# Value products with the values as weights, in two column groups, and attention outputs kept transposed

## What is computed

```python
def sb_block(q, q_pos, k, v, k_pos):
    z = jnp.einsum('bqhd,bkhd->bhqk', q, k) * SB_HD ** -0.5
    mask = (k_pos[None, :] < q_pos[:, None])[None, None]
    log_beta = jax.nn.log_sigmoid(z)
    l = jnp.where(mask, jax.nn.log_sigmoid(-z), 0.0)
    c = lax.cumsum(l, axis=3, reverse=True) - l
    w = jnp.where(mask, jnp.exp(log_beta + c), 0.0)
    return jnp.einsum('bhqk,bkhd->bqhd', w, v)
...
    mix = jnp.concatenate([og, o_sb.reshape(B, T, SB_WIDTH)], axis=-1).astype(x.dtype)
    h = x + mix @ w_out
    u = rmsnorm(h, norm2_g).astype(x.dtype) @ w_up
    return h + jnp.square(jax.nn.relu(u)) @ w_down
```

## Time and profile before

| | |
|---|---|
| median of 3 runs | 3177.38 us (3176.07 to 3178.87) |
| the profiled execution | 3173.07 us, with a span of 3171.3 us |
| PE busy | 3076.5 us of the span |
| DVE, ACT, POOL busy | 1893.9, 1693.8, 1107.1 us |
| value products, line 1471 | 2256 records, from 859.8 to 2844.7 us |
| mean granted clock | 0.986 |

### The profile page before, as it was taken

One profiled execution on the slowest core, in us unless ns is written; L12 is line 12 of the kernel. 1 busy time (PEld: TensorE's weight loads), 2 busy tenths in 40 slices (PEclk: granted clock), 3 DMA queues, 4 the chain that ended last, 5 costly groups with the idle time before them and its releaser, 6 DMA issues. The chain is left out here.

```text
span 3171.3 us, 48786 instructions
## 1 busy us (share of the span) xinstructions
PE 3076.5 (97%) x18258; PEld 2640.2 (83%) x18258; DVE 1893.9 (60%) x3388; ACT 1693.8 (53%) x3148; POOL 1107.1 (35%) x642
## 2 busy tenths in 40 slices
PE   6999999999779999999999999999999999999999
PEld 5887788877679989888888988888898888889998
DVE  2565646546446666566665776777757667653333
ACT  3443434443357766555555666666556655543443
POOL 0331513215135663333333232222333333334665
PEclk9999999999779999999999999999999999999999
DMA  4654645544455554323333323222233333333443
GB/s 148 185 176 140 193 132 161 155 138 114 147 156 176 182 177 128 113 86 104 101 91 115 107 97 99 91 92 89 81 126 115 133 98 102 98 99 120 133 145 111
DMA packets 310747, 400.66 MB, mean 126 GB/s; under 512 B 70433, under 2 KB 225074, under 8 KB 309490
## 3 DMA queue, kind: packets, MB, share of 16 engines
q1 hardware_dynamic: 310514, 397.55, 40.1%
HBM read 339.95 MB, written 57.54 MB: 125 GB/s over the span
## 5 line engine op out<-in xcount | busy, mean ns | idle before, releaser
L1861 POOL TENSOR_TENSOR st_ul<-st_ur,st_uh 128x1024 fp32r<-128x1024 f32 x180 | 428.8, 2404 | 803.4 <-ACT st_uh L1669 803.4
L1868 POOL TENSOR_TENSOR st_dl<-st_dr,st_dh 128x1024 fp32r<-128x1024 f32 x180 | 430.9, 2415 | 610.4 <-ACT st_dh L1679 610.4
L1835 DVE TENSOR_TENSOR st_ya<-st_ya,st_dp 128x512 f32<-128x512 f32 x544 | 368.6, 681 | 97.2 <-PE st_dp L1589 96.0
L1636 ACT ACTIVATE st_a<-st_z 128x512 f32<-128x512 f32 (+3 forms) x336 | 177.2, 527 | 380.9 <-PE st_z L1448 252.7
L1761 DVE TENSOR_TENSOR_SCAN st_g<-st_z,st_g,st_a 128x511 f32<-128x511 f32 (+3 forms) x336 | 371.0, 1104 | 15.6 <-DVE st_g L1754 0.5
L1822 DVE TENSOR_TENSOR st_tl<-st_dp,st_th 128x512 fp32r<-128x512 f32 (+2 forms) x168 | 96.8, 576 | 437.6 <-ACT st_dp L1717 437.5
L1589 PE MATMUL st_dp<-st_dh,st_th 128*128 128x512 f32 x1020 | 336.9, 402 | 0.7 <-DVE st_ya L1835 0.6
L1589 PE MATMUL st_dp<-st_dh,st_tl 128*128 128x512 f32 x1020 | 336.9, 401 | 0.0
L1589 PE MATMUL st_dp<-st_dl,st_th 128*128 128x512 f32 x1020 | 334.5, 399 | 0.0
L1471 PEld LDWEIGHTS st_po<-st_v,st_wt 128*128 128x128 f32 x2256 | 303.3, 194 | 36.2 <-DMA st_v<-out_new_v 7.6
L495 PE MATMUL fr_pj<-fr_wl,fr_xh 128*128 128x512 f32 x816 | 330.3, 405 | 0.0
(11 more groups left out here) (165 smaller groups left out, 5738.6 us busy)
## 6 DMA issues: line engine op xcount, KB each, us to landing
st_ur<-in_w_up SPq DMA_DIRECT2D x75, 1024.0 KB, 5.3
st_dr<-in_w_down SPq DMA_DIRECT2D x75, 1024.0 KB, 4.9
fr_wr<-in_w_in SPq DMA_DIRECT2D x96, 512.0 KB, 4.0
st_ur<-in_w_out SPq DMA_DIRECT2D x10, 1024.0 KB, 5.0
st_dr<-in_w_out SPq DMA_DIRECT2D x10, 1024.0 KB, 5.0
fr_xb<-in_x SPq DMA_DIRECT2D x17, 512.0 KB, 4.5
st_ya<-in_x SPq DMA_DIRECT2D x17, 512.0 KB, 7.3
out_y<-st_ya SPq DMA_DIRECT2D x16, 512.0 KB, 3.9
```

Source lines behind the costliest of these rows:

```text
L1835: dve.tensor_tensor(part, part, dp[:, k % BANKS], ALU.add).then_inc(s_fd, 1)
L1861: pool.tensor_tensor(ul[:, c], ur[:, c], raw(uh[:, c]), ALU.subtract).then_inc(s_ul, 1)
L1868: pool.tensor_tensor(dl[:, k], dr[:, k], raw(dh[:, k]), ALU.subtract).then_inc(s_dl, 1)
```

## The change

`values` swaps the operands: `v` is stationary (128 keys x 64 columns) and `wt` moves (128 keys x 128 queries), so `po` now holds 64 columns x 128 queries, transposed. Key tile c writes partitions 0 to 63 when c is even and 64 to 127 when it is odd (the array's two column groups), and the two halves are added afterwards. A pair with a single key tile does it twice, once per half. ACT's `output` becomes `other_half`: for head h it copies the half that does not lie at the partitions of h's place (parity of h) into `mv`. A new `output` on DVE adds the half still in `po` to `mv` and writes it to `mT`, already transposed, at that place. `s_of`, for which PE's next pair waits, now comes from DVE. `mix_tile` transposes `mg` only; ACT and DVE read the second half of `xh` and `xl` from `mT`, and `out_tile` waits for that by `s_ml`. `MG` goes from 4 to 3 buffers.

```diff
@@ settings and plan
-MG = 4
+MG = 3
...
-                for a in range(2):
+                for a in range(1 if kind == "mix" else 2):
...
@@ tensor, values(u)
                 for c in range(un.n):
-                    mm = pe.matmul(po[:, tt % 2 * HD:(tt % 2 + 1) * HD], wt[:, u % 3, c * P:(c + 1) * P],
-                                   v[:, p, un.e * jobs[un.job].keys + un.lo + c],
-                                   start=(un.first and c == 0), stop=(un.last and c == un.n - 1))
+                    for half in range(2) if un.first and un.last and un.n == 1 else (c % 2,):
+                        mm = pe.matmul(po[64 * half:64 * half + 64, tt % 2], v[:, p, un.e * jobs[un.job].keys + un.lo + c],
+                                       wt[:, u % 3, c * P:(c + 1) * P], start=(tt, half) not in begun, stop=(un.last and c >= un.n - 2))
+                        begun.add((tt, half))
                 mm.then_inc(s_pv, 1)
...
@@ tensor, out_tile
                 if gg == 0:
-                    pe.wait_ge(s_fd, plan.full("mix", b, j, 1))
+                    pe.wait_ge(s_fd, plan.full("mix", b, j, 0))
+                    pe.wait_ge(s_ml, rows_before[b] + j + 1)
...
@@ scalar, part 2 of u(3)
-            def output(u):
+            def other_half(u):
                 un = units[u]
                 if un.last:
                     tt = tiles_done[u]
-                    b = jobs[un.job].block
+                    q = un.h % 2
                     act.wait_ge(s_pv, u + 1)
-                    if b and tt == outs_done(b - 1):
-                        act.wait_ge(s_full, plan.full("mix", b - 1, MTS[b - 1] - 1, 1))
-                    act.activation(ms[:, un.tile, un.h * HD:(un.h + 1) * HD], po[:, tt % 2 * HD:(tt % 2 + 1) * HD], ACT.Copy).then_inc(s_of, 1)
+                    if tt >= 2:
+                        act.wait_ge(s_of, tt - 1)
+                    act.activation(mv[64 * q:64 * q + 64, tt % 2], po[64 - 64 * q:128 - 64 * q, tt % 2], ACT.Copy).then_inc(s_oc, 1)
...
@@ scalar, high_halves (second half of a mix tile)
+                                yield plan.done("mix", b, j, 0) + 1
+                                act.wait_ge(s_of, outs_done(b))
+                                act.activation(xh[:, 4:8, j * P:(j + 1) * P], mT[:, :, j * P:(j + 1) * P], ACT.Copy).then_inc(s_hi, 1)
...
@@ vector
+            def output(u):
+                un = units[u]
+                if un.last:
+                    tt = tiles_done[u]
+                    b = jobs[un.job].block
+                    q = un.h % 2
+                    dve.wait_ge(s_oc, tt + 1)
+                    if b and tt == outs_done(b - 1):
+                        dve.wait_ge(s_ml, rows_before[b])
+                    ps = slice(64 * q, 64 * q + 64)
+                    dst = mT[ps, un.h // 2, un.tile * P:(un.tile + 1) * P]
+                    if un.first and un.n == 1:
+                        dve.tensor_copy(dst, po[ps, tt % 2]).then_inc(s_of, 1)
+                    else:
+                        dve.tensor_tensor(dst, po[ps, tt % 2], mv[ps, tt % 2], ALU.add).then_inc(s_of, 1)
...
             def part0(u):
+                if u(4) is not None:
+                    output(u(4))
                 if u(2) is not None:
                     transposed(u(2))
```

More of the change, by code:

```diff
@@ L1190, in __init__ @@
         first = [self.start[self.use["mix", b, 0, 0]] for b in range(MB)]
-        last = [self.end[self.use["mix", b, 1 if b else MTS[0] - 1, 1]] for b in range(MB)]
+        last = [self.end[self.use["mix", b, 1 if b else MTS[0] - 1, 0]] for b in range(MB)]
         self.region = [(-100e3, 0.0)] + [(last[b], first[b + 1]) for b in range(MB - 1)]
@@ L1256, in phase_stream @@
         wt = m.sb("wt", [P, 3, 512])
-        ms = m.sb("ms", [P, MT, 512])
+        mT = m.sb("mT", [P, 4, MT * P])
+        mv = m.sb("mv", [P, 2, P])
         mg = m.sb("mg", [P, MG, 512])
@@ L1273, in phase_stream @@
         tp = m.ps("tp", [P, 512])
-        po = m.ps("po", [P, 512])
+        po = m.ps("po", [P, 2, P])
         dp = m.ps("dp", [P, BANKS, 512])
@@ L1279, in phase_stream @@
         s_gb = m.sem("gb")
+        s_oc, s_ml = m.sem("oc"), m.sem("ml")
         s_kq, s_v = m.sems("kq", 2), m.sems("v", 2)
@@ L1459, in transposes @@
                 mm.then_inc(s_tr, 1)
+            begun = set()
             def values(u):
@@ L1481, in mix_tile @@
                 t = rows_before[b] + j
[L1482 to L1493, removed]
+                k = plan.use["mix", b, j, 0]
+                yield plan.start[k]
+                free(k)
+                pe.wait_ge(s_mg[t % MG], 16 * (t // MG + 1))
+                for c in range(4):
+                    mm = pe.transpose(dp[:, k % BANKS, c * P:(c + 1) * P], mg[:, t % MG, c * P:(c + 1) * P], idt[:])
+                mm.then_inc(s_full, 1)
             def out_tile(b, gg, j):
@@ L1684, in high_halves @@
                         for a2 in range(2):
+                            if kind == "mix" and a2:
+                                yield plan.done("mix", b, j, 0) + 1
+                                act.wait_ge(s_of, outs_done(b))
+                                act.activation(xh[:, 4:8, j * P:(j + 1) * P], mT[:, :, j * P:(j + 1) * P], ACT.Copy).then_inc(s_hi, 1)
+                                continue
                             k = plan.use[kind, b, j, a2]
@@ L1728, in part2 @@
                 if u(3) is not None:
-                    output(u(3))
+                    other_half(u(3))
                 if u(-1) is not None:
@@ L1780, in low_halves @@
                         for a2 in range(2):
+                            n += 1
+                            if kind == "mix" and a2:
+                                yield plan.done("mix", b, j, 0) + 1
+                                dve.wait_ge(s_hi, n)
+                                dve.tensor_tensor(xl[:, 4:8, j * P:(j + 1) * P], mT[:, :, j * P:(j + 1) * P],
+                                                  raw(xh[:, 4:8, j * P:(j + 1) * P]), ALU.subtract).then_inc(s_ml, 1)
+                                continue
                             k = plan.use[kind, b, j, a2]
-                            n += 1
                             yield plan.end[k]
```

## The result

| | before | with the change |
|---|---|---|
| median of 4 runs | 3177.2 us | 3224.6 us (3221.8 to 3234.9) |
| ratio | 1 | 1.0155, 95% interval 1.0132 to 1.0177 |
| span of the profiled execution | 3171.3 us | 3222.2 us |

What follows compares the result with a forecast made beforehand. PE, in flight 97% of the span, was taken to bound the kernel. The terms -8.5 - 7.5 + 32 + 10 + 2 = +28 us on 3173.1 gave 3201 us, and with 4.3 us for the median 3205 us, range 3185 to 3225.

Steps and rivals of the forecast that it cites:

- Value groups: Value products on PE, blocks 1 to 4: 0.78 us a unit for 4 or 3 key tiles, 0.56 for fewer; -8.5 us.
- the switch: On PE, each value group pays 0.34 us for going from the whole array to parts of it and back.
- rival 3: Value products on PE: no switch cost with all 128 rows in use; about -85 us in all, 3092 us; chance 0.10.
- Transposes: Mix stages on PE: 17 mix tiles lose four transposes each, 0.43 to 0.44 us a group; -7.5 us.
- The new wait: Pair starts in blocks 1 to 4: PE's values wait for DVE's late addition; +32 us, bounds nothing and 47.
- Rival 1: Pair starts: DVE is in time, so its additions make PE wait little; near -10 us, 3167 us; chance 0.17.
- Block 0: Block 0's attention at half clock: waits for DVE at seven of 16 pairs and dearer value units; +10 us, bounds 3 and 13.
- MG = 3: Mix stages: a block's fourth mix tile's load waits for the first one's transposes; +2 us, bounds 0 and 5.

Runs made afterwards that it cites:

- a_half: The changed kernel with every key tile on the first column half, ACT copying that half and DVE only moving it: 3330 us in a single run, ratio 1.0496.
- a_pair: a_best with the values of two units in one group, every second slot, on PE, ACT and DVE: 3127.8 us, ratio 0.9853 to the kernel before.
- a_load: The changed kernel with the mix load of a block's fourth tile sent to an idle third of hn and issued early: ratio 1.0081 to the kernel before.
- a_best: The changed kernel with both the load edit of a_load and the copy edit of a_copy: ratio 0.9981 to the kernel before, from 11 runs.
- b_mg3: The kernel before with only MG changed from 4 to 3 buffers: ratio 1.0052, +16.5 us in the medians.
- b_dve: The kernel before with the copy of po to ms moved from ACT, part 2, to DVE, part 0 of the next slot: ratio 1.0125, +36.6 us in the medians.
- a_copy: The changed kernel with po emptied by ACT alone in part 2, PE waiting for that, and DVE adding afterwards: ratio 1.0055 to the kernel before.

## Why the prediction was right in sign and short in size

- **Value groups: right.** 0.78 and 0.56 us a unit were forecast and measured, for every size of unit. That the columns work side by side was taken from the earlier trace rows; a_half shows it. That the switch is paid on 128 rows too, so that rival 3 falls, is in the two groups above, and a_pair, with half as many switches, gets back most of what they cost.
- **Transposes: right.** -7.5 was forecast for 17 tiles, 6.6 of it for the 15 in the mix stages of the table, and a_load's are 7.3 us shorter with a wait that accounts for 0.6.
- **The new wait: right.** "Of the 40 us I take 0.8, +32 us." Rival 1 falls: in blocks 1 to 4 PE stands 24.9 us for the addition and 4.6 us with no engine named. What it costs was measured three times: 36.6 us when it is put alone into the kernel before, 32 us back when it is taken out of the change, and again 0.0100, 32 us, with the load repaired (a_load to a_best). Of the 24.9 us at least 15.6 lie in block 3; the prediction had 24.9 of its 40 us there.
- **Block 0: oversized.** +10 was forecast, the stage became 3.1 us longer (44.7 to 47.8), the lower bound given. PE does wait 9.2 us for DVE there, seven times as forecast. But before it had waited 5.4 us for ACT, 5.1 of it at the place where it now waits 4.3 for DVE, and the wait for the load of `st_v` became 0.8 us shorter.
- **MG = 3: the step that failed.** "I take **+2 us**, bounds 0 and 5; in blocks 2 and 3 three down tiles lie between and cover it." It measured 21.6 us in the mix stages and 23 us in the ratios (a_load). The prediction reckoned landing from the moment the load may leave, and left out SP's queue: there the load stands behind a weight load that waits for POOL, and behind five loads of attention. So it left 8 us late in block 1, and 8 to 9 us late in blocks 2 and 3, where the three down tiles don't cover it; PE waited 9.9, 5.0 and 6.2 us.
- **The clock in blocks 1 to 4: left out.** The sum has no term for it. By stages it forecast +10 us for block 0, -5 for the mix stages and +23.5 for the attention stretches; the changed kernel's trace has +3.1, +14.3 and +34.0. So the attention stretches missed by 10 us of their own, though the prices of their groups and the wait came out as forecast. From 946 us on the granted clock in them is 0.50 for 26.0 us in five pieces, three behind the waits for `st_mg`, one in a wait for the addition and one behind a wait for `st_xl`; in the kernel before it is 1.00 there all the time. That is worth up to 13 us (an estimate: half of the 26.0). The misses of the three stages, +19, +10 and -7 us, are the profiled execution's, 51 us where 28 were forecast. The sign rests on the new wait, which was right; that the sum came nearer than its two short terms is luck, since block 0, too high by 7 us, took part of them back.
- **What stays open.** Attention stretches of a_best are 2.2 us longer than before, where -8.5 was the term. PE's waits for `st_xl` are 4 us longer (7.3 against 3.4), and the granted clock is 0.50 from 1253.2 to 1256.6 and from 2383.0 to 2389.9 us, where before it was 1.00; that can be worth 5 us. Neither was tried by itself.

## What to carry to other kernels

Price a change of array shape by the group, not by the product: here half the array twice as fast gained 0.11 us on four key tiles, because 0.34 us went to leaving and re-entering the full array, and only putting two units into one group made the form pay. Where a release moves from one engine to another, read how late that engine is at the new place, start by start; its mean idle time (40% here) didn't show it. And with one buffer less, ask not when the load may leave but what stands ahead of it on its queue.

## What the runs showed that I had not expected

The clock fell with the wait for mg. Windows of the changed kernel, with TensorE's granted clock as the column after PE's busy time:

```profile
1187.40:1191.50 4.10, 0.00 (x1) 1.00 0.68 213
1191.50:1201.70 10.20, 4.39 (x21) 0.50 1.01 339
1201.70:1206.00 4.30, 4.30 (x36) 0.99 0.01 3
```

PE stood from 1187.4 us on. From 1191.5 to 1201.7 the granted clock was 0.50, that is 1.2 GHz, so the transposes after the wait took 1.09 instead of 0.60 us. The same is seen in b_mg3 (1.09 at 1193.14). In the mix stages little of it is beyond the waits themselves (15.8 and 21.6 us, with 15.0 and 21.2 us of waiting); but the low clock goes on into the attention stretches behind them.

The new wait does the same. In the changed kernel PE stands at a pair start in block 3, and the clock falls in that wait:

```profile
2250.77 0.69 PE L1476 MATMUL st_po<-st_wt,st_v 128*64 128x128 f32 x4 [3.16 <-DVE st_mT L1796]
...
2249.70:2256.50 6.80, 5.73 (x17) 0.50 0.96 332
2434.00:2440.80 6.80, 5.92 (x18) 0.50 0.75 241
```

The third row is a stretch of block 4's attention, where PE stands 2.35 us for `st_xl` just before. Half clock in the midst of block 3's attention (between 2237 and 2257 us) is seen in the three kernels in which PE waits for DVE there, the change, a_load and b_dve, and in none of the kernel before, b_mg3, a_copy, a_best and a_pair. So some of PE's waits here cost more than their own length: the work behind them runs slower. That the wait brings the clock down is read from where the two stand, and from which kernels have both; the clock wasn't changed by itself. The mean granted clock says it for the whole kernel, 0.977 to 0.981 in the four runs of the change against 0.986 before.
